# Sparse attention: order of the query parts, the key compression and the second key transposes

## The chip, the cores and the metric

One core of a Trainium2 chip runs the whole program in one launch. The metric is the device time of an execution in microseconds (us), lower is better. PE is TensorE, DVE is VectorE, ACT is ScalarE, POOL is GpSimd, and SP is SyncE, which issues the weight loads.

## The reference

The input x has 256 positions of width 1024 in float32. Three layers with a feed-forward part each are computed: a first block of forgetting attention and retention, then a layer of sparse attention (`nsa_pool_mixer`) with a pooling mixer, then a gated linear attention layer. The change lies in the sparse attention only. What it computes, for 8 query heads in 2 key groups of head dimension 64:

```python
h = x @ w_in                      # queries, six key/value sets, gates, u
kc = compress_blocks(k_cmp, ...)  # gelu(flat @ w1 + b1) @ w2: 15 compressed keys
vc = compress_blocks(v_cmp, ...)
p_c = masked_softmax(qb @ kc, ...);  o_c = p_c @ vc      # branch over compressed keys
p_s = masked_softmax(qb @ k_sel, ...); o_s = p_s @ v_sel # branch over selected blocks
p_w = masked_softmax(qb @ k_w, ...);  o_w = p_w @ v_w    # branch over the window
o = g0 * o_c + g1 * o_s + g2 * o_w
```

With 256 positions the selected blocks and the window both cover all keys, so both of these branches are causal attention over 256 keys, with different key sets.

## The kernel before

Every large product runs in three matmul passes, over a high and a low part of both factors: hi x hi, lo x hi, hi x lo. Weights stream in tiles of 128 x 1024 (512 KB) into a ring of 6 raw slots (SP, `fetch_w`). ACT makes the high part `whi` of each tile (line 600), DVE the low part `wlo` (line 1137), also in rings of 6, and PE uses both (lines 1816 to 1818, 12 matmuls for a tile of 256 input rows). The low part of a tile frees its raw slot for the next load.

The sparse attention's input product takes 16 such tiles, T_AIN + 0 to T_AIN + 15, four for each block of output columns: keys and values of compression and selection (tiles 0 to 3), queries (4 to 7), window keys, values and gates (8 to 11, 280 columns), and u (12 to 15). The work of the attention itself is written by hand between these tiles. Each engine has a table `between` (PE) or `tiles(...)` (ACT and DVE) whose entry n lists the steps that follow tile n in program order. On ACT and DVE the entry n comes after the high or low part of tile n + 3, except for entries 12 to 14, which come before it. Every engine runs its list in order, and semaphores alone join the lists.

The names that the change touches:

- `nsa_transposes(f)` on PE (line 2292): four 128 x 128 transposes into bank 2 or 3 of the PSUM tensor AT. f = 0, 1 are the keys and values to be compressed, 2 the window keys' set for the first branch, 3 to 6 the queries (position half t, head half j), 7 the second set of keys. f = 7 writes bank 2, and waits until DVE has copied the turned probabilities of group 6 out of it (`at_trd`). f = 5 and 6 wait until the low part before the last was taken from their bank (`nt_lo`).
- `nt_out(f)`, `q_out(f)` on ACT (line 941): copy of the transposed bank to SBUF as high part. `q_low(f)`, `k_low(f)` on DVE (lines 1547, 1553): its low part, read from the same bank.
- `compress` on PE (line 2320) is the product with w1, `hidden_bias` on ACT adds b1, `gelu_start` on DVE begins the gelu. `gelu_exp` on ACT (line 959) is the exponential in it, the first since other functions were used, so a table load stands with it. `gelu_end` on DVE (lines 1563 to 1567) ends it. `compress2` on PE (lines 2326, 2327) waits for it and forms the compressed keys and values. `compressed_out` on DVE (lines 1575 to 1580) copies them out.
- `cmp_scores` on PE (line 2336) are the scores on the compressed keys, `cmp_max` on DVE (to line 1604), `cmp_exp` on ACT (line 970) and `cmp_probs` on DVE (from line 1608) are their softmax, `cmp_transposes` on PE turns it.
- Groups 6 to 17 are the softmax groups of the other two branches. For group n: `S_(n)` scores on PE (lines 2041, 2052), always in bank 1 of AT, so that it waits for the exponentials of group n - 1; `maxima(n)` on DVE (line 1376); `exps(n)` on ACT (line 811); `weigh(n)` on DVE (lines 1622 to 1626); `T_(n)` transposes on PE (line 2065) into bank 2; `probs_out(n)` on DVE (line 1384), the copy out of it; `V_(n)` values on PE (lines 2390, 2394). Group 6 needs all four query parts (`nt_lo` at 5), and `T_(7)` waits for `k_low(7)` (`nt_lo` at 6), because both use bank 2.

Of the kernel before, what the change touches and what calls it, by code (L numbers as in the profile page):

```python
# [12 lines left out]
P = 128  # L13
# [157 lines left out]
def block_program(nc, dram, out):  # L171
    with ExitStack() as ctx:
        def sb(name, shape, dt=F32):
            return ctx.enter_context(nc.sbuf_tensor(name, shape, dt))
# [22 lines left out]
        kst = sb("kst", [P, 4, 512], F32R)  # L197
# [116 lines left out]
        K_HI = (2, 0)  # L314
# [18 lines left out]
        def rows_of(t):  # L333
            return slice(t * P, (t + 1) * P)
# [246 lines left out]
        def _(act):  # L581
# [221 lines left out]
            def exps(n):  # L803

                br, t, heads = GROUPS[n]
                act.wait_ge(at_max, n + 1)
                if n >= 2:
                    act.wait_ge(at_tr, n - 1)
                w = 512 // len(heads)
                for u, h in enumerate(heads):  # L810
                    ins = nc.scalar.activation(pr[:, n % 2, u * w:(u + 1) * w], AT[:, S_BANK[n], u * w:(u + 1) * w],
                                               ACT.Exp, bias=nmax[:, n % 2, u:u + 1],
                                               accum_out=rsum[:, t, 8 * br + h:8 * br + h + 1])
                ins.then_inc(at_exp, 1)
# [122 lines left out]
            def nt_out(f, dst, n=64):  # L937

                act.wait_ge(nt_tr, f + 1)
                b = AT[0:n, 2 if f == 7 else 2 + f % 2, :]  # L940
                nc.scalar.activation(dst, b if len(dst.shape) == 2 else b.rearrange("d (h s) -> d h s", h=4),
                                     ACT.Copy).then_inc(nt_done, 1)

            def q_out(f):
                t, j = (f - 3) // 2, (f - 3) % 2
                nt_out(f, q_tile(j, t), P)
# [47 lines left out]
            def nsa_hi(t):  # L994
# [9 lines left out]
                4: [lambda f=f: nt_out(f, kT[:, f * 512:(f + 1) * 512], P) for f in range(2)],  # L1004
                5: [lambda: nt_out(2, kst[:, K_HI[0], :], P)],
                7: [queries_out, hidden_bias],
                8: [gelu_exp] + [lambda f=f: q_out(f) for f in (3, 4)],
                9: [lambda f=f: q_out(f) for f in (5, 6)],
                10: [lambda: exps(6)],
                11: [window_out, branch_gates, lambda: exps(7)],  # L1010
                12: [lambda: exps(8)],
                13: [cmp_exp, lambda: nt_out(7, kst[:, K_HI[1], :], P), lambda: exps(9)],
                14: [cmp_out, lambda: exps(10)],
                15: [u_out, lambda: exps(11), means_out, lambda: exps(12), pooled_hi, lambda: exps(13)],
            }, range(12, 15))
# [94 lines left out]
        def _(dve):  # L1110
# [56 lines left out]
            def tiles(s0, s1, after, first=()):  # L1167


                for s in range(s0, s1):  # L1170
                    if s - s0 not in first:
                        raw_to(raw_of(s + LEAD) + 1)
                    for step in after.get(s - s0, ()):
                        step()
                    lo_to(s + LEAD)
# [194 lines left out]
            def maxima(n):  # L1370

                u = len(GROUPS[n][2])
                dve.wait_ge(at_mm, n + 1)
                if n >= 2:
                    dve.wait_ge(at_exp, n - 1)
                nc.vector.tensor_reduce(nmax[:, n % 2, 0:u], AT[:, S_BANK[n], :].rearrange("p (u k) -> p u k", u=u),
                                        AX, ALU.max, negate=True).then_inc(at_max, 1)
# [164 lines left out]
            def q_low(f):  # L1542

                t, j = (f - 3) // 2, (f - 3) % 2
                dve.wait_ge(nt_done, f + 1)
                own = q_tile(j, t)[64:P]
                tt(own, AT[64:P, 2 + f % 2, :].rearrange("d (h s) -> d h s", h=4), own.bitcast(F32), ALU.subtract)\
                    .then_inc(nt_lo, 1)

            def k_low(f, br):  # L1550

                dve.wait_ge(nt_done, f + 1)
                tt(kst[:, K_HI[br] + 1, :], AT[:, 2, :], kst[:, K_HI[br], :].bitcast(F32), ALU.subtract).then_inc(nt_lo, 1)
# [80 lines left out]
            def pooled_lo():  # L1634
# [4 lines left out]
                        hT_hi[:, 4 + g, :].bitcast(F32), ALU.mult, ALU.subtract).then_inc(pl_lo, 1)  # L1639

            tiles(T_AIN, T_AOUT, {
                5: [block_keys, lambda: k_low(2, 0)], 7: [gelu_start], 8: [gelu_end, lambda: q_low(3), lambda: q_low(4)],
                9: [compressed_out, lambda: q_low(5), lambda: q_low(6)],
                10: [lambda: maxima(6)],
                11: [gates_out, lambda: weigh(6), lambda: maxima(7)],
                12: [lambda: maxima(8), lambda: probs_out(6), lambda: weigh(7), cmp_max],
# [145 lines left out]
        def _(pe):  # L1792
# [353 lines left out]
            def fox_values(n):  # L2146

                if n == 0:
                    pe.wait_ge(bank_free[1], 4)
                if n == 2:  # L2150
                    pe.wait_ge(at_out, 1)
                _, t, heads = GROUPS[n]
                pe.wait_ge(at_trd, n + 1)
                b = 0
                for h in heads:
                    for kt in range(t + 1):
                        ins = mm(AT[:, 3, 64 * h:64 * h + 64], prT[:, n % 2, b * P:(b + 1) * P],
                                 proj[:, kt, FV + 64 * h:FV + 64 * (h + 1)], start=kt == 0, stop=kt == t)
                        b += 1
                ins.then_inc(at_pv, 1)  # L2160
# [53 lines left out]
            S_, T_, V_ = fox_scores, prob_transposes, fox_values  # L2214
# [77 lines left out]
            def nsa_transposes(f):  # L2292

                if f < 3:
                    pe.wait_ge(bank_free[0], 2 * (B_AIN // 2) + 2)
                    srcs = [acc[:, KD + 256 * t + P * g:KD + 256 * t + P * (g + 1)] for g in range(2) for t in range(NT)]
                    if f < 2:
                        srcs = [proj[:, t, KDUP + P * (2 * f + g):KDUP + P * (2 * f + g + 1)] for g in range(2) for t in range(NT)]
                elif f < 7:
                    t, j = (f - 3) // 2, (f - 3) % 2  # L2300
                    pe.wait_ge(bank_free[1], 2 * ((B_AIN + 1) // 2) + 2)
                    srcs = [acc[:, QD + D * t + P * (4 * j + a):QD + D * t + P * (4 * j + a + 1)] for a in range(4)]
                else:
                    pe.wait_ge(bank_free[0], 2 * ((B_AIN + 2) // 2) + 2)
                    pe.wait_ge(at_trd, NF + 1)
                    srcs = [acc[:, KD + 256 * t + P * g:KD + 256 * t + P * (g + 1)] for g in range(2) for t in range(NT)]
                if 2 <= f < 7:
                    pe.wait_ge(nt_done, f - 1)
                if 4 <= f < 7:
                    pe.wait_ge(nt_lo, f - 3 if f > 4 else 1)  # L2310
                for c, a in enumerate(srcs):
                    ins = nc.tensor.transpose(AT[:, 2 if f == 7 else 2 + f % 2, c * P:(c + 1) * P], a, ident)
                ins.then_inc(nt_tr, 1)
# [16 lines left out]
            def cmp_scores(tiles):  # L2330
                pe.wait_ge(c2_done, 3)
                pe.wait_ge(nt_lo, 5)
                for t in tiles:
                    for h in range(8):
                        for part in range(2):
                            ins = mm(AT[:, 0, 256 + P * t + 16 * h:256 + P * t + 16 * (h + 1)],
                                     q_stack(h)[:, rows_of(t)],
                                     kcst[:, part, h // 4, :], start=part == 0, stop=part == 1)
                ins.then_inc(cs_mm, 1)
# [72 lines left out]
            def pool_mix():  # L2412

                pe.wait_ge(pm_done, 2)
                for g in range(4):
                    ins = mm(PJ[:, 2 + g // 2, (g % 2) * S:(g % 2 + 1) * S], acc[:, POOLW + P * g:POOLW + P * (g + 1)],
                             proj[:, 1, RT_ + S * g:RT_ + S * (g + 1)], start=True, stop=True)
                    if g % 2:
                        ins.then_inc(py_mm, 1)

            S_, T_, V_ = nsa_scores, nsa_probs, nsa_values
# [3 lines left out]
                9: [lambda: nsa_transposes(5), lambda: nsa_transposes(6), compress2],  # L2425
                10: [lambda: S_(6)],
                11: [lambda: S_(7), lambda: cmp_scores((0,))],
                12: [lambda: T_(6), lambda: S_(8), lambda: cmp_scores((1,))],
                13: [lambda: V_(6), lambda: nsa_transposes(7), lambda: S_(9), lambda: T_(7)],
                14: [lambda: V_(7), cmp_transposes, lambda: T_(8), lambda: S_(10)],  # L2430
                15: [cmp_values, lambda: V_(8), lambda: T_(9), lambda: S_(11), pool_bands, lambda: V_(9), lambda: T_(10), lambda: S_(12),
                     pool_mix, lambda: V_(10), lambda: T_(11), lambda: S_(13)],
            }
            mixer(B_AIN, T_AIN, 3, quarters(3, from_x, (2, 3), [(mod_row, 8)]), [n for _, n in A_IN], between)
            between = {0: [lambda: V_(11), lambda: T_(12), lambda: S_(14)],
                       1: [lambda: V_(12), lambda: T_(13), lambda: S_(15)],
# [149 lines left out]
```

## Time and profile before

| | us |
|---|---|
| runs of the kernel before | 991.39, 990.47, 992.85 (median 991.39) |
| the profiled execution | 991.15 |
| its span, first to last instruction | 989.2 |
| the sparse attention's tiles and steps | about 380 to 475 of the span |

The profile gives the busy time of each engine and a chain of work that ended last, followed back from the last instruction. A timeline lists the instructions of an engine in order of time, those alike merged, with the idle time ahead of them and what ended it in brackets. Of the matmuls the starts are measured and the ends modelled, so distances are best taken from start to start. The granted clock is the share of TensorE's full clock of 2.4 GHz.

### The profile page before, as it was taken

What the parts mean: (1) busy time and instruction counts of PE and PEld (TensorE: products, weight loads), DVE (VectorE), ACT (ScalarE), POOL (GpSimd) and SP (SyncE); (2) the same over time, 40 slices, a digit from 0 to 9 for tenths busy, and PEclk for the clock granted to TensorE, in tenths of its full rate; (3) what the DMA queues carried; (4) which work ended last, traced back from release to release, by engine and by line L of the source; (5) the groups of instructions that cost most, each with busy time, mean ns of one, the idle gap of its engine ahead of it and who ended that gap; (6) DMA issues with size and microseconds to landing.
All of it is one profiled execution on the core that took longest, in us unless ns stands there. A gap on an engine that the chain in (4) does not pass through costs nothing.

```text
span 989.2 us, 13707 instructions
## 1 busy us (share of the span) xinstructions
PE 958.2 (97%) x4982; PEld 797.0 (81%) x4982; DVE 675.2 (68%) x875; ACT 463.4 (47%) x710; POOL 55.0 (6%) x61
## 2 busy tenths in 40 slices
PE   9999999999999999899899999998999999999996
PEld 7778877888888887777688888887776888888885
DVE  5868898895566576677976556667643876655657
ACT  5477535464445345544355444444652434544441
POOL 3040111200000001000200000000000010000000
PEclk9999999999999999999999999999999999999998
DMA  9979787596555676421375665564342537566541
GB/s 303 336 227 276 220 255 235 198 313 210 194 170 193 206 258 165 128 86 46 121 246 192 196 204 174 190 211 153 127 148 86 168 132 233 193 197 205 170 148 43
DMA packets 110053, 186.91 MB, mean 189 GB/s; under 512 B 8729, under 2 KB 67169, under 8 KB 109985
## 3 DMA queue, kind: packets, MB, share of 16 engines
q1 hardware_dynamic: 104800, 177.33, 55.1%
q0 software_dynamic: 2656, 8.54, 3.2%
q8 instruction: 32, 0.52, 0.2%
q10 hardware_dynamic: 2544, 0.35, 0.2%
q14 instruction: 21, 0.16, 0.1%
HBM read 185.15 MB, written 1.05 MB: 188 GB/s over the span
## 4 chain that ended last, share of the span: by engine, by line
PE 78%; DVE 11%; ACT 3%; issue 3%; DMA 2%; POOL 2%; SPq 0%; POOLq 0%; DVEq 0%; ACTq 0%
PE AT L1956 16%; PE PJ L1816 14%; PE PJ L1817 14%; PE PJ L1818 14%; PE AT L1960 8%; DVE wlo L1137 3%; POOL rstd L483 2%; ACT whi L600 1%; PE AT L1802 1%; DVE bn L1225 1%; DMA raw<-in_w_out_dram 1%; DMA raw<-in_w_ada_dram 1%; PE AT L1816 1%; PE AT L2065 1%; DVE x L1223 1%
## 5 line engine op out<-in xcount | busy, mean ns | idle before, releaser
L1137 DVE TENSOR_TENSOR wlo<-raw,whi 128x1024 fp32r<-128x1024 f32 x144 | 173.4, 1221 | 50.9 <-ACT whi L600 50.1
L1956 PE MATMUL AT<-hT,whi 128*128 128x512 f32 x720 | 179.5, 391 | 0.0
L1263 DVE TENSOR_TENSOR wlo<-raw,whi 128x1024 fp32r<-128x1024 f32 x144 | 169.6, 1219 | 0.0
L600 ACT ACTIVATE whi<-raw 128x1024 fp32r<-128x1024 f32 x144 | 146.6, 1054 | 40.1 <-DMA raw<-in_w_in_dram 28.8
L1816 PE MATMUL PJ<-whi,uhi 128*128 128x512 f32 x392 | 154.0, 393 | 0.4
L1817 PE MATMUL PJ<-wlo,uhi 128*128 128x512 f32 x392 | 153.0, 390 | 0.0
L1818 PE MATMUL PJ<-whi,ulo 128*128 128x512 f32 x392 | 152.6, 389 | 0.0
L1956 PEld LDWEIGHTS AT<-hT,whi 128*128 128x128 f32 x720 | 131.9, 188 | 25.3
L1816 PE MATMUL PJ<-whi,hT 128*128 128x512 f32 (+1 forms) x360 | 146.7, 407 | 4.7 <-DVE hT L1320 1.6
L1273 DVE TENSOR_TENSOR pr<-AT,pr 128x512 f32<-128x512 f32 x45 | 31.1, 691 | 169.0 <-ACT pr L655 169.0
L647 ACT ACTIVATE whi<-raw 128x1024 fp32r<-128x1024 f32 x144 | 140.7, 1049 | 0.3 <-DMA raw<-in_mlp_w_dram 0.3
L1817 PE MATMUL PJ<-wlo,hT 128*128 128x512 f32 (+1 forms) x360 | 139.6, 388 | 0.0
L1818 PE MATMUL PJ<-whi,hT 128*128 128x512 f32 (+1 forms) x360 | 139.5, 388 | 0.0
L655 ACT ACTIVATE pr<-AT 128x512 f32<-128x512 f32 x45 | 26.8, 595 | 173.4 <-PE AT L1960 173.4
L1960 PEld LDWEIGHTS AT<-hT,wlo 128*128 128x128 f32 x720 | 98.2, 190 | 7.0
L1960 PE MATMUL AT<-hT,wlo 128*128 128x256 f32 x720 | 100.4, 282 | 0.0
L1818 PEld LDWEIGHTS PJ<-whi,ulo 128*128 128x128 f32 x392 | 73.6, 188 | 15.7
L1816 PEld LDWEIGHTS PJ<-whi,hT 128*128 128x128 f32 x360 | 68.2, 189 | 22.2 <-issue 4.8
L1816 PEld LDWEIGHTS PJ<-whi,uhi 128*128 128x128 f32 x392 | 73.7, 188 | 15.2 <-issue 1.2
L1817 PEld LDWEIGHTS PJ<-wlo,uhi 128*128 128x128 f32 x392 | 73.8, 188 | 13.8 <-issue 0.2
L1818 PEld LDWEIGHTS PJ<-whi,hT 128*128 128x128 f32 x360 | 68.0, 189 | 14.4
L1817 PEld LDWEIGHTS PJ<-wlo,hT 128*128 128x128 f32 x360 | 68.2, 189 | 13.0 <-issue 1.0
(332 smaller groups left out, 995.9 us busy)
## 6 DMA issues: line engine op xcount, KB each, us to landing
raw<-in_mlp_w_dram SPq DMA_DIRECT2D x128, 512.0 KB, 4.8
raw<-in_w_in_dram SPq DMA_DIRECT2D x32, 512.0 KB, 6.4
raw<-in_w_ada_dram SPq DMA_DIRECT2D x32, 512.0 KB, 5.6
raw<-in_w_mlp_in_dram SPq DMA_DIRECT2D x32, 512.0 KB, 4.9
raw<-in_w_mlp_out_dram SPq DMA_DIRECT2D x32, 512.0 KB, 4.7
raw<-in_c_w_in_dram SPq DMA_DIRECT2D x24, 512.0 KB, 4.5
raw<-in_w_ada_dram SPq DMA_DIRECT2D x32, 256.0 KB, 6.6
raw<-in_a_w_in_dram SPq DMA_DIRECT2D x12, 512.0 KB, 5.2
```

Of the source, the lines that this page charges most:

```text
L483: nc.gpsimd.tensor_tensor(rstd[:, col:col + n], stat[:, col:col + n], nhalf[:, 0:n], ALU.pow).then_inc(rstd_ready, 1)
L600: nc.scalar.activation(whi[:, s % SPL, :], raw_slot(r), ACT.Copy).then_inc(hi_done, 1)
L647: nc.scalar.activation(whi[:, s % SPL, :], raw_slot(r), ACT.Copy).then_inc(hi_done, 1)
L655: nc.scalar.activation(pr[:, 0, :].rearrange("p (f s) -> p f s", f=2), AT[:, up_banks(j), S:], ACT.Copy).then_inc(cross_out, 1)
L1137: tt(wlo[:, n % SPL, :], raw_slot(r), whi[:, n % SPL, :].bitcast(F32), ALU.subtract).then_inc(raw_done, 1)
L1263: tt(wlo[:, s % SPL, :], raw_slot(r), whi[:, s % SPL, :].bitcast(F32), ALU.subtract)\
L1273: tt(z, AT[:, up_banks(j), 0:S], z, ALU.add).then_inc(up_out, 1)
L1816: mm(o, a, hi, start=start, stop=False)
L1817: mm(o, a, lo, start=False, stop=False)
L1818: return mm(o, b, hi, start=False, stop=stop)
L1956: mm(out(f), whi[:, s % SPL, c(kk, f)], hT[:, k, :, :].rearrange("p a s -> p (a s)"), start=k == 0, stop=False, skip_group_check=True)
L1960: ins = mm(out(f)[:, 0:S], wlo[:, s % SPL, c(kk, f)], hT_hi[:, k, :], start=False, stop=k == KC - 1, skip_group_check=True)
```

## The change

Three tables are reordered. On ACT, entry 8 runs the copies of query parts 3 and 4 before the gelu's exponential, and entry 13 the copy of the second set of keys before the exponential of the compressed scores. On DVE, entry 8 takes the low parts of query parts 3 and 4 before `gelu_end`, and entry 9 those of parts 5 and 6 before `compressed_out`. On PE, the transposes of the second set of keys go from entry 13, behind the values of group 6, to the end of entry 12, ahead of tile 13. No instruction is added or removed.

```diff
@@ ACT
-                8: [gelu_exp] + [lambda f=f: q_out(f) for f in (3, 4)],
+                8: [lambda f=f: q_out(f) for f in (3, 4)] + [gelu_exp],
                 9: [lambda f=f: q_out(f) for f in (5, 6)],
                 10: [lambda: exps(6)],
                 11: [window_out, branch_gates, lambda: exps(7)],
                 12: [lambda: exps(8)],
-                13: [cmp_exp, lambda: nt_out(7, kst[:, K_HI[1], :], P), lambda: exps(9)],
+                13: [lambda: nt_out(7, kst[:, K_HI[1], :], P), cmp_exp, lambda: exps(9)],
@@ DVE
-                5: [block_keys, lambda: k_low(2, 0)], 7: [gelu_start], 8: [gelu_end, lambda: q_low(3), lambda: q_low(4)],
-                9: [compressed_out, lambda: q_low(5), lambda: q_low(6)],
+                5: [block_keys, lambda: k_low(2, 0)], 7: [gelu_start], 8: [lambda: q_low(3), lambda: q_low(4), gelu_end],
+                9: [lambda: q_low(5), lambda: q_low(6), compressed_out],
@@ PE
-                12: [lambda: T_(6), lambda: S_(8), lambda: cmp_scores((1,))],
-                13: [lambda: V_(6), lambda: nsa_transposes(7), lambda: S_(9), lambda: T_(7)],
+                12: [lambda: T_(6), lambda: S_(8), lambda: cmp_scores((1,)), lambda: nsa_transposes(7)],
+                13: [lambda: V_(6), lambda: S_(9), lambda: T_(7)],
```

## Rows read from the trace of the kernel before

**Rows 1.** The page: busy time and share of PE; chain that ended last, by engine.

```profile
PE 958.2 (97%) x4982; PEld 797.0 (81%) x4982; DVE 675.2 (68%) x875; ACT 463.4 (47%) x710; POOL 55.0 (6%) x61
...
PE 78%; DVE 11%; ACT 3%; issue 3%; DMA 2%; POOL 2%; SPq 0%; POOLq 0%; DVEq 0%; ACTq 0%
```

**Rows 2.** PE's waits, 385 to 475 us: what for; us, times, longest.

```profile
PE AT L2312 <- DVE uhi L1547: 1.0, 1, 1.0
PE AT L2041 <- DVE ulo L1547: 0.9, 1, 0.9
```

**Rows 3.** Timeline of ACT: start, duration, instruction, idle before and releaser.

```profile
403.01 1.28 ACT L959 ACT_TABLE_LOAD   x1
404.31 0.25 ACT L959 ACTIVATE sc<-sc 64x60 f32<-64x60 f32 x1
404.47 0.58 ACT L941 ACTIVATE uhi<-AT 128x512 fp32r<-128x512 f32 x1
404.94 0.58 ACT L941 ACTIVATE ulo<-AT 128x512 fp32r<-128x512 f32 x1
...
407.37 0.60 ACT L941 ACTIVATE uhi<-AT 128x512 fp32r<-128x512 f32 x1 [0.90 <-PE AT L2312]
...
426.01 0.40 ACT L970 ACTIVATE proj<-proj 128x240 f32<-128x240 f32 x1 [1.49 <-DVE proj L1604]
```

**Rows 4.** Timeline of DVE, same columns.

```profile
404.59 0.18 DVE L1563 TENSOR_SCALAR sc<-sc 64x60 f32<-64x60 f32 x1 [0.34 <-ACT sc L959]
...
405.86 0.69 DVE L1547 TENSOR_TENSOR uhi<-AT,uhi 64x512 fp32r<-64x512 f32 x1
...
407.19 1.23 DVE L1137 TENSOR_TENSOR wlo<-raw,whi 128x1024 fp32r<-128x1024 f32 x1
408.55 0.17 DVE L1575 CAST kcst<-nhalf 128x4 fp32r<-128x4 f32 x1
...
412.42 0.69 DVE L1376 TENSOR_REDUCE nmax<-AT 128x4 f32<-128x512 f32 x1
...
421.83 0.69 DVE L1376 TENSOR_REDUCE nmax<-AT 128x2 f32<-128x512 f32 x1 [2.39 <-PE AT L2052]
422.44 0.68 DVE L1384 COPY prT<-AT 128x512 f32<-128x512 f32 x1
...
428.18 0.69 DVE L1553 TENSOR_TENSOR kst<-AT,kst 128x512 fp32r<-128x512 f32 x1 [1.06 <-ACT kst L941]
...
429.62 0.69 DVE L1384 COPY prT<-AT 128x512 f32<-128x512 f32 x1 [0.15 <-PE AT L2065]
```

**Rows 5.** Timeline of PE, same columns.

```profile
403.12 1.03 PE L2312 MATMUL AT<-cst,acc 128*128 128x128 f32 x8
...
406.70 1.24 PE L2312 MATMUL AT<-cst,acc 128*128 128x128 f32 x8 [1.01 <-DVE uhi L1547]
407.87 0.40 PE L2326 MATMUL AT<-sc,nsm 64*128 64x30 f32 x2
...
414.70 0.39 PE L2041 MATMUL AT<-negb,identb 128*128 128x512 bf16 x1 [0.74 <-ACT pr L811]
...
423.33 0.48 PE L1816 MATMUL PJ<-whi,hT 128*128 128x512 f32 x1
...
427.38 0.72 PE L2052 MATMUL AT<-kst,uhi 128*128 128x256 f32 x4
428.92 0.66 PE L2065 MATMUL AT<-cst,pr 128*128 128x128 f32 x4 [0.83 <-DVE kst L1553]
```

**Rows 6.** Windows: length, busy PE, PEld, DVE, ACT, POOL; granted clock; DMA share, GB/s.

```profile
133.00:136.00 3.00, 0.93 (x6) 0.53 (x6) 2.60 (x6) 0.60 (x1) 0.00 (x0) 1.00 0.56 214
136.00:140.00 4.00, 4.00 (x17) 3.61 (x18) 4.00 (x4) 2.74 (x4) 0.00 (x0) 0.57 0.41 117
70.00:72.00 2.00, 0.19 (x4) 0.00 (x0) 1.09 (x2) 0.92 (x1) 2.00 (x3) 1.00 0.30 115
72.00:76.00 4.00, 3.76 (x22) 3.20 (x23) 3.76 (x5) 3.10 (x3) 0.45 (x1) 1.00 0.79 211
```

## The prediction

> **What bounds the kernel now.** I read the engine table of the page first: PE is busy for 958.2 us of the span, 97% [rows 1]. The chain that ended last lies on PE for 78% and on DVE for 11% [rows 1]. So a change of order on ACT and DVE can only win where PE waits for one of them. The list of PE's waits between 385 and 475 us, the stage that the diff touches, and then the bracketed idle times in PE's own timeline name four such stops: 1.0 us in front of transposes for DVE's `q_low`, 0.9 us in front of group 6's scores for `q_low` [rows 2], 0.74 us in front of group 7's scores for ACT's exponentials, and 0.83 us in front of a transpose for `k_low` [rows 5]. That is 3.5 us, 0.35% of the run, and the most that this change could return here. The timelines of ACT, DVE and PE around these four stops give the order behind each [rows 3 to 5]. "Tile n" is weight tile T_AIN + n, "group n" a softmax group.
>
> **First part: `gelu_exp`, `gelu_end` and `compressed_out` go behind the `q_out`/`q_low` pairs.** Nothing is added or removed; the same instructions stand in another order. Before, ACT runs the table load (1.28 us from 403.01), the exponential (404.31), then `q_out(3)` and `q_out(4)` (404.47, 404.94) [rows 3]. DVE runs `gelu_end` from 404.59, `q_low(3)` and `q_low(4)` from 405.86, the low part of tile 12 from 407.19, `compressed_out` from 408.55, then `q_low(5)`, `q_low(6)`, the low part of tile 13, and the maxima of group 6 at 412.42 [rows 4].
>
> ACT in the new order. PE's transposes 3 and 4 start at 403.12 [rows 5]. From the start of such transposes to the copy that reads them it is 0.67 us (406.70 to 407.37) [rows 3, 5], so `q_out(3)` starts at 403.79. `q_out(4)` follows 0.47 later, the pitch of this pair when both inputs are there (404.47 to 404.94) [rows 3]: 404.26, end 404.84 with its 0.58. Load and exponential keep their distances (403.01 to 404.31 is 1.30) [rows 3]: the load starts at 404.86, the exponential at 406.16.
>
> DVE in the new order. `q_low(3)` runs from 404.39 and `q_low(4)` to about 405.7, so PE's transposes 5 and 6 start when tile 9 ends, 1.01 us (their stop) sooner than 406.70 [rows 5]: this stop is gone. But `gelu_end` starts 0.28 behind the exponential (404.31 to 404.59) [rows 3, 4], at 406.44, and ends 1.24 later at 407.68. PE's `compress2` waits for it and stood at 407.87 before [rows 5]: it gains only 0.1 us. The first stop isn't removed; it moves behind the two transposes (1.17 us from 405.69) and is there near 1 us again. On DVE, `gelu_end` is 1.85 later than 404.59; the pair's 1.33 (405.86 to 407.19) no longer stands behind it; and the gap of 0.13 between the low part of tile 12 (end 407.19 + 1.23) and 408.55 closes [rows 4]. So everything from there on is 1.85 - 1.33 - 0.13 = 0.39 later, the maxima of group 6 too: 412.8 in place of 412.42. I take +0.38.
>
> The scores of group 6 do come sooner: `q_low(6)` ends at 406.44 + 1.27 + 1.26 + 1.31 = 410.3, by the pitches of `gelu_end`, a low part and a pair [rows 4], so PE wins about 0.8 of the second stop. It has nothing to spend it on. After tile 11 it must issue the scores of group 7 into the same bank, and these wait for the exponentials of group 6, which wait for the maxima, which stand on DVE behind the low part of tile 13 whatever the scores do. From the maxima at 412.42 to the scores at 414.70 [rows 4, 5] all shifts by +0.38. The stop of 0.74 grows to 0.74 + 0.8 + 0.38 = 1.9 us. **First part: a loss of 0.38 us.**
>
> The bounds. If `q_out(4)` came 0.60 after `q_out(3)`, the length of a copy as at 407.37 [rows 3], it would be 0.51; if the table load stayed in front of the copies, `gelu_end` would start behind the `q_low` pair at 406.24, a loss of 0.2. I take the pitch of 0.47 as it is the same two copies. If PE's 0.8 us counted after all, the part would be a gain of 0.8. What is queued behind the later steps: on ACT the high part of tile 12, about 1.0 later, on DVE its low part, 0.5 later than 407.19 [rows 4], which PE needs at tile 12, behind the scores of group 7 at 414.70 [rows 5]; on SP the fetch into the slot that this low part frees, 0.5 later too, and in this stage PE waits for no DMA [rows 2]. All are costed at nothing; with the cover gone they would cost 0.5. POOL has no step here. From 414.70 to tile 13 at 423.33 PE's timeline shows no stop [rows 5], since what it waits for shifts alike, so the 0.38 is carried there whole.
>
> The Trainium skill, ScalarE: Activation LUTs, section "Step-by-step: what each stage is for", says that the load of a table set stands right before the activation that needs it; the row agrees (403.01, 404.31) [rows 3]. The same page, section "What ACT_TABLE_LOAD costs", adds a drain of 1.38 us to a load of 1.28. The row shows the load, and ACT not idle ahead of it [rows 3]; with that drain the first part would cost 1.76 us, an estimate by that page.
>
> **Second part: `nsa_transposes(7)` goes from behind tile 13 to ahead of it, and `nt_out(7)` ahead of `cmp_exp`.** In its new place it waits on PE for DVE's copy of group 6's turned probabilities, which leaves bank 2 of AT free. That copy ends at 422.44 + 0.68 = 423.12, and PE starts tile 13 at 423.33 [rows 4, 5]; both carry the same +0.38. PE starts 0.15 behind such a releaser (405.86 + 0.69 = 406.55 to 406.70) [rows 4, 5], so it would start at 423.27: cost 0, at most 0.1. Queued behind this wait is all of tile 13. The four transposes take as long in either place. ACT copies them in its hole of 1.49 us ahead of `cmp_exp` (426.01) [rows 3], and DVE's `k_low(7)` starts as soon as the low part of tile 15 ends, 1.06 sooner than 428.18 [rows 4]. On PE, the scores of group 9 stay at 427.38, since the transposes only changed sides of tile 13, and group 7's transposes lose their stop of 0.83 [rows 5]. DVE sets what comes next: its maxima of group 9 start 0.04 after the scores' end at 427.38 + 0.72 [rows 5], at 428.14, the copy 0.61 later (421.83 to 422.44) at 428.75, against 429.62 [rows 4]: 0.87. Its softmax over the compressed keys and its weighing hang on that copy, and PE's next transposes on them. Bounds 0.83 and 0.95. **Second part: a gain of 0.87 us.**
>
> **Sum.** 0.38 - 0.87 = -0.49 us, say -0.5. The profiled execution took 991.15 us (the span of 989.2 and 1.95 around it), the runs shown have a median of 991.39. On the profile's base that is 990.65, on the median's 990.9.
>
> **The rivals.**
> - *The scores' head start counts in full.* The first part is then a gain of 0.8, and the sum -1.7: 989.7. It needs the maxima at 411.6, and against that stands DVE's queue, which has no hole from 406.44 on. Chance 0.07.
> - *The second set's transposes stall.* If the copy out of bank 2 came so late that the stop only moved ahead of tile 13, the second part would give nothing: +0.4, 991.8. For it: the margin is under 0.1 us. Chance 0.08.
> - *A drain at the table load.* The exponential would come another 1.38 later, and the sum be +0.9: 992.3. Against it: no gap stands ahead of 403.01 [rows 3]. Chance 0.06. The page named above is what speaks for it.
> - *TensorE's clock falls.* The place is the two stops that the new order makes, over 1 us near 406.4 and 1.9 us near 413.2. Between 133 and 136 us PE was busy for 0.93 of 3 us, and the granted clock over the next 4 us was 0.57, mostly the 1.2 GHz level [rows 6]: (1 - 0.57) x 4 = 1.7 us lost. Against it: between 70 and 72 us PE was busy for 0.19 of 2 us, and the clock stayed at 1.00 [rows 6]. [...] One fall gives -0.5 + 1.7 = +1.2: 992.6, chance 0.15. A fall at each stop gives +2.9: 994.3, chance 0.04. This is the case that ends slower.
>
> **Numbers.** The forecast has 0.60. The range goes from 989.7, the first rival, to 992.9, one fall with 0.3 of scatter; outside are the double fall and the tails. About 0.2%, 2.0 us, is what a measurement here can tell from no change. Only the double fall, or one fall with a drain or with scatter, gets there: slower 0.08. Faster by 2.0 us would need the first rival with scatter: 0.05. Within: 0.87.
>
> **What would show it.** ACT's table load at 404.9 behind two copies; PE's transposes 5 and 6 an us sooner and a stop in front of `compress2`, which is near 407.8; the scores of group 6 at 410.3; group 7's at 415.1, with a stop near 1.9 for ACT; the copy for `k_low(7)` ahead of `cmp_exp`; group 7's transposes at 428.3 in place of 428.92 [rows 5], with no stop for `k_low(7)`. A granted clock under 1.00 between 407 and 420, a table load ahead of the copies, maxima of group 6 before 412.4, or a stop in front of `nsa_transposes(7)` would each make the sum wrong.

## The result, and the profile after

| | kernel before | changed kernel |
|---|---|---|
| median of 18 runs, us | 992.42 | 995.22 |
| lowest and highest, us | 989.95, 994.93 | 990.63, 998.12 |
| profiled execution, us | 991.15 | 996.75 |
| its span, us | 989.2 | 994.8 |
| its mean granted clock | 0.993 | 0.987 |

The changed kernel is slower by 0.24%: the ratio is 1.0024, 95% interval 1.0013 to 1.0035, that is 2.4 us with 1.3 to 3.5. The forecast of 990.9 us had its range end at 992.9, and 995.22 lies outside.

The waits of PE in this stage come first (385 or 388 us to 480; what waits for what; us in total, times, longest). After:

```profile
PE AT L2041 <- ACT pr L811: 1.7, 1, 1.7
PE AT L2326 <- DVE proj L1567: 1.2, 1, 1.2
PE AT L2065 <- issue: 0.9, 3, 0.4
PE PJ L1816 <- DVE hT L1638: 0.4, 1, 0.4
```

The two waits of [rows 2] are gone, and so is the 0.83 for `k_low` in [rows 5]. In their place stand 1.2 us in front of `compress2` and 1.7 in front of group 7's scores (0.74 before). Both were forecast. The listed waits are shorter than before as a sum, so they don't say where 2.4 us went. The windows do (start and end; length; busy time of PE, PEld, DVE, ACT, POOL; granted clock; DMA share; GB/s):

```profile
410.00:412.00 2.00, 0.84 (x7) 0.66 (x6) 1.90 (x5) 2.00 (x4) 0.00 (x0) 1.00 0.32 120
412.00:416.00 4.00, 3.91 (x30) 3.66 (x31) 3.87 (x9) 0.81 (x1) 0.00 (x0) 1.00 0.42 131
416.00:419.00 3.00, 1.30 (x12) 1.05 (x10) 0.67 (x2) 2.30 (x9) 0.00 (x0) 1.00 0.50 173
419.00:423.00 4.00, 4.00 (x22) 4.00 (x22) 3.64 (x8) 1.31 (x6) 0.00 (x0) 0.53 0.34 114
423.00:426.00 3.00, 3.00 (x8) 2.32 (x9) 0.00 (x0) 1.50 (x8) 0.00 (x0) 0.50 0.07 25
426.00:430.00 4.00, 4.00 (x32) 3.71 (x31) 1.56 (x5) 0.90 (x4) 0.00 (x0) 0.99 0.00 0
```

Behind the stop of 1.7 us the granted clock is at 0.50, the 1.2 GHz level, from 419 to 426 us. PE is fully busy there, at half the clock. In the profile of the kernel before, the clock was 1.00 through the whole stage. The product of time and missing clock is 0.47 x 4 + 0.50 x 3 + 0.01 x 4 = 3.4 us. I call this the clock loss below; for a whole run it is (1 - mean granted clock) x span. In this stage a stretch at 0.50 (a fall) has, in every profile that shows one, a clock loss of either 1.7 us, a single fall, or 3.4 us, a double one.

PE's timeline after, around this stop (start, duration, instruction, idle before):

```profile
406.67 1.04 PE L2312 MATMUL AT<-cst,acc 128*128 128x128 f32 x8
...
411.28 0.40 PE L2326 MATMUL AT<-sc,nsm 64*128 64x30 f32 x2 [1.16 <-DVE proj L1567]
...
413.75 0.39 PE L2041 MATMUL AT<-negb,identb 128*128 128x512 bf16 x1
...
418.26 0.39 PE L2041 MATMUL AT<-negb,identb 128*128 128x512 bf16 x1 [1.70 <-ACT pr L811]
418.30 1.29 PE L2052 MATMUL AT<-kst,ulo 128*128 128x128 f32 x8
419.39 1.82 PE L2336 MATMUL AT<-kcst,uhi 128*128 128x16 f32 x8
421.06 1.85 PE L2336 MATMUL AT<-kcst,ulo 128*128 128x16 f32 x8
422.77 0.77 PE L1816 MATMUL PJ<-whi,hT 128*128 128x512 f32 x1
```

Eight matmuls of the compressed scores (line 2336) take 1.82 us here. The start of the stage itself is 3.55 us later than before (406.67 against 403.12 in [rows 5]). That lies in code that the change doesn't touch, and most of it goes with falls of the clock at other places: ahead of this stage the changed kernel's profile has four single falls, that of the kernel before two. So the stage is measured from the start of the transposes of query parts 3 and 4. The three marks that I use rest on these rows, with [rows 5] and the timeline above. Before:

```profile
411.15 0.39 PE L2041 MATMUL AT<-negb,identb 128*128 128x512 bf16 x1 [0.91 <-DVE ulo L1547]
411.19 1.19 PE L2052 MATMUL AT<-kst,uhi 128*128 128x128 f32 x8
...
437.32 1.95 PE L2360 MATMUL AT<-proj 120*128 120x128 f32 x16
```

After:

```profile
442.88 1.95 PE L2360 MATMUL AT<-proj 120*128 120x128 f32 x16
```

| from the start of transposes 3 and 4, us | before | after |
|---|---|---|
| scores of group 6 | 8.03 | 7.08 |
| scores of group 7 | 11.58 | 11.59 |
| values of the compressed branch (line 2360, behind tile 15) | 34.20 | 36.21 |

### The profile page after: what moved, and what is told of

Its sections match the earlier page's. It is cut to its first block, busy times and chain, and to the rows that moved or that the text cites. A ratio compares the mean times of both kernels' runs of the same rounds, so it can differ in the third digit from the quotient of the medians.

```text
span 994.8 us, 13707 instructions
## 1 busy us (share of the span) xinstructions
PE 963.5 (97%) x4982; PEld 802.3 (81%) x4982; DVE 674.5 (68%) x875; ACT 463.4 (47%) x710; POOL 55.0 (6%) x61
## 4 chain that ended last, share of the span: by engine, by line
PE 79%; DVE 11%; issue 3%; ACT 3%; DMA 2%; POOL 2%; SPq 0%; POOLq 0%; DVEq 0%; ACTq 0%
PE AT L1956 16%; PE PJ L1816 14%; PE PJ L1817 14%; PE PJ L1818 14%; PE AT L1960 8%; DVE wlo L1137 3%; POOL rstd L483 2%; ACT whi L600 1%; PE AT L1802 1%; DMA raw<-in_w_out_dram 1%; DVE bn L1225 1%; PE AT L2065 1%; DMA raw<-in_w_ada_dram 1%; DMA raw<-in_w_in_dram 1%; PE AT L1816 1%
```

## The experiments

Theory **"clock"**: the new order makes a long stop in front of group 7's scores, TensorE's clock falls behind it, and this costs more than the order brings. Rival **"queues alone"**: the order costs time through DVE or ACT, and the fall is chance. All kernels were run with 12 timed runs each, beside 17 to 35 of the kernel before on the same chip. The last two columns are of the one profiled execution: the clock loss between 412 and 427 us, and the distance to the values of the compressed branch.

| kernel | median, us | ratio to before (95%) | mean clock loss of the runs, us | fall in the stage, us | distance, us |
|---|---|---|---|---|---|
| before (116 runs) | 992.75 | | 8.3 | 0 | 34.20 |
| changed (18 runs) | 995.22 | 1.0024 (1.0013 to 1.0035) | 11.9 | 3.4 | 36.21 |
| e10 changed, again | 993.49 | 1.0025 (1.0009 to 1.0041) | 11.1 | 3.4 | 36.20 |
| e1 first part only | 995.05 | 1.0019 (1.0003 to 1.0035) | 10.4 | 3.4 | 37.22 |
| e2 second part only | 992.62 | 0.9998 (0.9982 to 1.0014) | 9.5 | 0 | 33.23 |
| e3 scores' stop filled | 991.94 | 0.9992 (0.9976 to 1.0009) | 8.6 | 1.7 | 34.57 |
| e4 maxima first | 991.38 | 0.9991 (0.9971 to 1.0010) | 9.6 | 1.7 | 33.60 |
| e5 before, delayed | 995.88 | 1.0037 (1.0022 to 1.0052) | 10.8 | 3.4 | 38.26 |
| e6 before, delayed, filled | 995.17 | 1.0018 (1.0003 to 1.0033) | 8.8 | 1.7 | 36.61 |
| e7 compress2's stop filled | 993.98 | 1.0022 (1.0005 to 1.0039) | 11.3 | 1.7 | 34.55 |
| e8 candidate | 991.79 | 0.9992 (0.9977 to 1.0006) | 9.0 | 0 | 32.29 |
| e9 both stops filled | 992.58 | 1.0004 (0.9990 to 1.0019) | 9.4 | 1.7 | 34.56 |
| e11 second part, filled | 990.57 | 0.9983 (0.9965 to 1.0001) | 7.3 | 0 | 33.22 |
| e12 before, filled | 992.76 | 0.9997 (0.9980 to 1.0014) | 7.9 | 1.7 | 35.50 |

The mean clock loss has a standard error of 0.5 to 0.9 us for 12 runs, 0.2 for the 116 of before. No version is shown to be faster than the kernel before: no interval lies wholly below 1.

### The parts alone: e1 and e2

e1 takes the ACT entry 8 and the DVE entries 8 and 9 of the change, e2 the ACT entry 13 and the PE entries.

> Only the first part: the exponential of the gelu behind query copies 3 and 4 on ScalarE, gelu_end and compressed_out behind the low parts on VectorE; the second set of keys stays where it was. Theory 'clock': the stop of PE in front of group 7's scores grows from 0.7 to about 1.7 us, the granted clock falls to half behind it as in the changed kernel (from 419 to 426 there), and that costs about 3.4 us: 992.4 + 0.4 + 3.4 = 996.2 us, 0.4% slower than before. Theory 'queues alone': the maxima of group 6 are 0.4 us later, no more, the clock is as before: 992.8 us, the same.

Measured: 995.05 us, ratio 1.0019; that is 1.2 us under what "clock" expected, and the kernel is slower than before, which "queues alone" did not expect. The stop and the fall are those of the changed kernel, in PE's timeline and in the windows of e1:

```profile
418.49 0.39 PE L2041 MATMUL AT<-negb,identb 128*128 128x512 bf16 x1 [1.71 <-ACT pr L811]
```

```profile
419.00:423.00 4.00, 4.00 (x23) 4.00 (x22) 3.41 (x8) 1.55 (x6) 0.00 (x0) 0.54 0.28 92
423.00:427.00 4.00, 4.00 (x13) 3.22 (x13) 0.23 (x1) 1.51 (x8) 0.00 (x0) 0.60 0.11 41
```

> Only the second part: the transposes of the second set of keys one step up on PE, their copy ahead of cmp_exp on ScalarE. Both theories: the stop of 0.83 us in front of group 7's transposes is gone, the stop in front of group 7's scores stays at 0.74, no fall of the clock in this stage: 992.4 - 0.9 = 991.5 us. If the second part itself were what brings the loss, it would be 994 or more.

Measured: 992.62 us, no difference by the runs; the 0.9 that was expected is inside the interval (1.6 us to each side). The order itself shows in the trace without scatter: the distance to the compressed values is 33.23 us in place of 34.20, a gain of 0.97, and no fall in the stage. So the loss is in the first part, and its profile has the fall: its distance of 37.22 us is 34.20 + 3.02, so by order it gives or takes nothing.

### Filling the stops: e3, e7, e9

A filler is a matmul of constants, 128 x 256, 0.44 us, into a bank of AT that nobody uses at that point (`busy`). It changes no other instruction. e3:

```diff
-                11: [lambda: S_(7), lambda: cmp_scores((0,))],
+                11: [lambda: busy(3, 3), lambda: S_(7), lambda: cmp_scores((0,))],
```

> The changed kernel with three matmuls of 256 columns on constants, written to an unused bank, ahead of group 7's scores on PE, so that PE works in the stop of 1.7 us. Theory 'clock': no fall of the clock near 419, time 995.2 - 3.4 = 991.8 us, as the forecast of the queues alone has it (-0.5 against before). Theory 'queues alone' (the loss is a delay on DVE or ACT): the fillers save nothing, 995.2 us; and if they stood in the way of the scores, up to 0.3 more.

Measured: 991.94 us. The scores of group 7 stand at 11.60 us behind the transposes, so the fillers cost nothing, and the stop has shrunk to 0.4. The runs' mean clock loss is 8.6 us, against 8.3 before and 11.6 in the 30 runs of the changed kernel. That is what "clock" expects, and "queues alone" is out: with the order unchanged, some 3 us come back. But the profiled execution still has a fall, a single one, and it starts later, some 3.9 us behind the start of group 7's scores in place of 0.9:

```profile
411.00:415.00 4.00, 3.61 (x26) 3.11 (x24) 2.25 (x3) 1.71 (x9) 0.00 (x0) 1.00 0.49 158
415.00:419.00 4.00, 4.00 (x30) 3.77 (x30) 3.06 (x8) 1.90 (x6) 0.00 (x0) 0.97 0.33 92
419.00:423.00 4.00, 4.00 (x17) 3.13 (x16) 0.58 (x1) 1.50 (x8) 0.00 (x0) 0.61 0.24 87
```

Its loss is 0.03 x 4 + 0.39 x 4 = 1.7 us, half of the changed kernel's. The fillers don't rule out every fall in this stage.

e7 has fillers in the other stop alone:

```diff
-                9: [lambda: nsa_transposes(5), lambda: nsa_transposes(6), compress2],
+                9: [lambda: nsa_transposes(5), lambda: nsa_transposes(6), lambda: busy(1, 2), compress2],
```

> The changed kernel with two matmuls on constants ahead of compress2, in the stop of 1.16 us, and none ahead of group 7's scores. If the clock falls by the stop in front of group 7's scores alone, it still falls: 995.2 us. If it takes both stops together, this filling is worth as much as the other one was: 992 us.

Measured: 993.98 us, between the two that were expected; but the ratio is 1.0022 and the mean clock loss 11.3, as in the changed kernel. The stop in front of `compress2` went from 1.16 to 0.29, the one of 1.7 stayed, and by the runs the loss stayed too. So the stop in front of group 7's scores is the one that counts. Its profile, of the fastest of its runs, has a single fall that starts 2.9 us behind the start of group 7's scores, not the double one, so the stop near 410 may have a share; one profile doesn't settle it.

> The changed kernel with fillers in both stops: two matmuls on constants ahead of compress2, three ahead of group 7's scores, order unchanged. From the traces, the order alone is worth -1.0 us (first part 0.0, second -1.0), so with the clock of the kernel before (0.992): 992.7 - 1.0 = 991.7 us. Theory 'clock': that. If the changed order cost time by a way of its own, filling wouldn't bring it under 994.

e9 joins both edits. Measured: 992.58 us, 0.9 above what was expected and 0.6 above e3; mean clock loss 9.4 with an error of 0.7. It is under 994, but doesn't beat e3, so filling `compress2`'s stop brings nothing more that these runs can tell.

### The stop made by hand in the old order: e5, e6

```diff
-                10: [lambda: maxima(6)],
+                10: [lambda: nc.vector.tensor_reduce(dly[:, :], x[:, 0, :], AX, ALU.max), lambda: maxima(6)],
```

> The kernel before, with one extra reduction of 128 x 1024 on VectorE (about 1.1 us, into a word that nobody reads) ahead of the maxima of group 6; nothing else is changed. It makes the stop in front of group 7's scores some 1.1 us longer (0.74 to 1.85), as long as in the changed kernel, without any of its reordering. Theory 'clock': the mean granted clock is lower than in the kernel before by about as much as in the changed one (0.003), so that the time rises by more than the delay: 992.8 + 1.1 + 3 = 997, with a fall of the clock between 415 and 425 in the profile. Rival 'no tie between this stop and the clock': 992.8 + 1.1 = 993.9 us and the clock of the kernel before.

> The same with three matmuls on constants (0.44 us each) ahead of group 7's scores. The delay stays, the stop is filled. Theory 'clock': only the delay is left, 993.9 us, and the mean granted clock is that of the kernel before (0.992). Rival: no difference from the one without the fillers.

Measured: 995.88 and 995.17 us. In e5 the scores of group 7 come 1.07 us later than before, and the windows show the fall (PE's timeline, then the windows; line numbers are one higher in this kernel):

```profile
414.73 0.39 PE L2042 MATMUL AT<-negb,identb 128*128 128x512 bf16 x1 [1.82 <-ACT pr L812]
```

```profile
412.00:415.00 3.00, 1.18 (x10) 0.93 (x9) 1.13 (x2) 1.83 (x9) 0.00 (x0) 1.00 0.51 175
415.00:419.00 4.00, 4.00 (x24) 4.00 (x22) 3.17 (x8) 1.78 (x6) 0.00 (x0) 0.57 0.22 68
419.00:423.00 4.00, 4.00 (x13) 3.26 (x13) 0.46 (x1) 1.50 (x8) 0.00 (x0) 0.57 0.17 64
```

The distance of 38.26 us is 34.20 + 1.07 of delay + 2.99: the price of a double fall, in an order that nobody changed. Other pairs of profiles agree: 3.02 between e1 and before, 2.98 between the changed kernel and e2 for a double fall, 1.30 to 1.35 (e12 and before, e4 and e8, e3 and e11) for a single one. e6 keeps the delay and fills the stop; its fall is single and its distance 36.61, that is 34.20 + 1.07 + 1.34. The mean clock loss of the runs is 10.8 us unfilled, 8.8 filled, 8.3 in the kernel before. e5 is what "clock" expected, 1 us less. e6 was expected at 993.9 and came 1.3 higher in the median (0.9 in the mean); the clock loss fell as forecast, the time only partly, and the rest I can't place. By their times alone the two aren't told apart: the ratios' intervals overlap, and the means differ by 1.4 us with a standard error of 0.8. The clock loss differs by 2.0 with an error of 0.7.

### Taking the stop away by the order: e4 and e8

```diff
-            }, range(12, 15))
+            }, (10, 12, 13, 14))
```

in DVE's table: with entry 10 in this list, `maxima(6)` stands ahead of the low part of tile 13.

> The changed kernel with one more move on VectorE: the maxima of group 6 ahead of the low part of tile 13 instead of behind it. Theory 'the low part of tile 13 stands in the way': the maxima come 1.1 us sooner against the scores of group 6, the stop in front of group 7's scores shrinks from 1.7 to about 0.6 us, the clock doesn't fall there, and the time is 991.8 - 1.1 = 990.7 us. Rival 'the stop is set by something else': the stop stays near 1.7, the clock falls, 995.2 us.

Measured: 991.38 us. The stop is 0.75, and the scores of group 7 are at 10.63 in place of 11.59 (timelines of DVE and of PE):

```profile
412.75 0.69 DVE L1376 TENSOR_REDUCE nmax<-AT 128x4 f32<-128x512 f32 x1
413.36 1.22 DVE L1137 TENSOR_TENSOR wlo<-raw,whi 128x1024 fp32r<-128x1024 f32 x1
```

```profile
415.04 0.39 PE L2041 MATMUL AT<-negb,identb 128*128 128x512 bf16 x1 [0.75 <-ACT pr L811]
```

It was DVE's queue that stood between the early scores of group 6 and their use, as the prediction had it. The time is 0.7 us above what was expected, and that the clock doesn't fall in the stage didn't come: a single fall is in this profile, from 2.9 us behind the start of group 7's scores.

> The changed kernel, with the maxima of group 6 ahead of the low part of tile 13 on VectorE, two matmuls on constants ahead of compress2 and one ahead of group 7's scores. By the queues: -1.8 us against the kernel before (first part +0.4, second -0.9, maxima -1.2), by the clock nothing lost: 992.8 - 1.8 = 991.0 us or a little less, with no fall of the clock between 400 and 425. Rival 'the clock falls here whatever fills the stops' (a fall was seen in the profile of the version with fillers ahead of the scores alone): 991.4 as without the fillers, mean clock 0.990.

e8 adds two fillers ahead of `compress2` and one ahead of group 7's scores. Measured: 991.79 us, 0.8 above the expected. No fall in the stage, and the shortest distance of all, 32.29 us, 1.91 under the kernel before. Over the whole run only about 1 us of it is seen, ratio 0.9992 (0.9977 to 1.0006). The profiled execution is the fastest of the twelve, 988.63 us at a mean clock of 0.995, and the twelve have 0.991; so that the fillers keep the clock up in the other runs isn't shown, and the rival (991.4 us, 0.990) isn't ruled out.

### Repeat, and the fillers in the old order: e10, e11, e12

> The changed kernel itself once more, beside the others on one chip, for the mean granted clock and the place of the falls: 995.2 us, mean clock 0.988 against 0.992 of the kernel before, and a fall between 415 and 427 us.

Measured: 993.49 us, 1.7 under the expected median; the mean is 994.45, against 992.49 of the kernel before on that chip. The ratio is 1.0025, the mean clock 0.989, and again there is the double fall at the same place, in its windows:

```profile
412.00:416.00 4.00, 2.30 (x19) 2.05 (x18) 1.66 (x2) 2.30 (x9) 0.00 (x0) 1.00 0.42 136
416.00:420.00 4.00, 4.00 (x23) 3.90 (x23) 3.64 (x8) 1.31 (x6) 0.00 (x0) 0.58 0.33 105
420.00:424.00 4.00, 4.00 (x12) 3.14 (x11) 0.00 (x0) 1.50 (x8) 0.00 (x0) 0.57 0.07 26
```

The distance is 36.20, after 36.21 in the first profile: with the clock's part known, the stage repeats within 0.01 us.

> Only the second part, with the three stops of the old order filled: two matmuls on constants ahead of the transposes of query part 5, one ahead of group 6's scores, one ahead of group 7's. By the queues 992.7 - 1.0 = 991.7 us. If falls in this stage also hit the kernel before in some of its runs, filling its stops gives a little more: the clock rises over 0.992, and the time is 991 or less. If not, it is the same as without fillers.

> The kernel before in its own order, with the same four fillers in its three stops as in the last one (two ahead of the transposes of query part 5, one ahead of group 6's scores, one ahead of group 7's). It parts the gain of 1.8 us of that version (990.9 mean against 992.7) into order and clock. If the kernel before loses clock in this stage in some of its runs, the mean granted clock rises over 0.992 and the time falls to about 992; if it doesn't, both stay: 992.7 us, clock 0.9917. The order alone is no faster here: nothing is moved.

e11 is the second part and `busy(1, 2)` ahead of transposes 5, `busy(1, 1)` ahead of group 6's scores, `busy(3, 1)` ahead of group 7's; e12 has the fillers without the second part. Measured: 990.57 us and 992.76 us. e12 is the kernel before within its scatter, clock loss 7.9 against 8.3, and its profile even has a single fall between 418 and 423 us. So filling the old stops brings nothing that can be told, and the single fall isn't bound to a stop in front of group 7's scores, which is 0.31 us here. e11 has the lowest median of all, ratio 0.9983 (0.9965 to 1.0001): the second part's 1.0 us by the trace, and a low clock loss that may be chance. It beats the changed kernel; that it beats the kernel before isn't shown, since its interval just reaches past 1.

## Why the prediction was wrong

**The mechanism was in it, with the wrong chance.** The rival "TensorE's clock falls" named the place, the stop in front of group 7's scores. It got 0.15 for one fall and 0.04 for two, and the sum put the clock at nothing. In the profiles, each of the two executions of the changed kernel has a double fall there, and so has e1, which shares the order of the first part, and e5, which shares only the stop. The 30 timed runs of the changed kernel have a mean clock loss of 11.6 us against 8.3. The step that failed is this term, left at nothing on the evidence against it: that between 70 and 72 us PE was busy for 0.19 of 2 us "and the clock stayed at 1.00" [rows 6]. This was one execution. In the profile of the changed kernel the same stop, in code that no edit touches, is 2.04 us long (PE's timeline), and this time the clock falls (windows):

```profile
74.15 1.57 PE L2132 MATMUL AT<-cst,proj 128*64 128x128 f32 x8 [2.04 <-DVEq L1361]
```

```profile
70.00:74.00 4.00, 2.11 (x14) 1.09 (x13) 2.13 (x5) 2.83 (x4) 4.00 (x4) 1.00 0.57 208
74.00:78.00 4.00, 3.85 (x14) 3.22 (x15) 3.81 (x4) 2.90 (x3) 0.37 (x1) 0.57 0.77 210
```

This stop is 2.04 to 2.06 us long in all 14 profiles. The clock falls behind it (between 72 and 78 us) in eight and holds in six. Behind the stop of 1.66 us near 136, whose fall [rows 6] shows, it falls in ten and holds in four. So such a stop is a risk that some executions pay and others don't, and one profile in which it isn't paid says little of the chance.

**What belongs to the long stop.** With a stop of at most 0.75 us in front of group 7's scores, none of the nine profiles has a double fall in the stage; five have a single one, which starts 2.4 to 3.9 us behind the start of these scores. With a stop of 1.7 to 1.8 us left open, four of five have a double fall, which starts within 0.7 to 1.4 us of them. So what the long stop brings is the early, double fall. What brings the later, single one no run here shows.

**The price of a fall.** The 1.7 us of [rows 6] is right as a unit: it comes once or twice in each fall. The prediction priced a fall per stop, two of them at 3.4 us, which with the order's -0.5 gave its +2.9. What came was a double fall behind one stop. In time it costs 2.99 us (e5) and a single one 1.34 (e6), less than the clock loss; the likely reason, not tested, is that not all of PE's time in it scales with the clock.

**The first part: 0.38 us forecast, 0.0 measured.** Group 7's scores are at 11.58 before and 11.59 after. ACT's side came as worked out: table load and exponential behind both copies, `gelu_end` at 409.99, which is 3.32 behind the transposes, as forecast (406.44 - 403.12). The mis-sized term is what follows on DVE. Its timeline after:

```profile
411.01 0.21 DVE L1567 COPY proj<-sc 64x120 f32<-64x120 f32 x1
411.15 1.21 DVE L1137 TENSOR_TENSOR wlo<-raw,whi 128x1024 fp32r<-128x1024 f32 x1
412.39 0.69 DVE L1547 TENSOR_TENSOR uhi<-AT,uhi 64x512 fp32r<-64x512 f32 x1
...
413.72 0.17 DVE L1575 CAST kcst<-nhalf 128x4 fp32r<-128x4 f32 x1
...
414.85 1.22 DVE L1137 TENSOR_TENSOR wlo<-raw,whi 128x1024 fp32r<-128x1024 f32 x1
415.98 0.68 DVE L1376 TENSOR_REDUCE nmax<-AT 128x4 f32<-128x512 f32 x1
```

The maxima start 1.13 us behind the low part of tile 13. The prediction shifted the whole queue rigidly from 412.42 on [rows 4], as if the maxima had stood there for DVE. In the kernel before they stand 1.30 behind the low part of tile 13 (from 411.12) and had waited for the scores of group 6, whose matmuls end at 412.38 (411.19 + 1.19, above); that distance was a wait and not DVE's pitch. In e5 the extra reduction, which needs nothing of PE, starts 1.14 behind the same low part. With the scores early these 0.17 us close up. Two more distances are shorter with another instruction behind them: from the last step of `gelu_end` to the next instruction 0.14 in place of 0.24, and from the start of `compressed_out` to what follows it 1.13 in place of 1.24. Why, the runs don't show. Together that is 0.38 us, the whole of the forecast's loss.

**The second part: 0.87 forecast, 0.97 measured** (34.20 to 33.23 in e2), just over its upper bound of 0.95. The missing 0.10 is in "The four transposes take as long in either place": from their start to the next instruction it is 0.41 us ahead of tile 13 (e2) and was 0.50 behind the values of group 6, so the scores of group 9 come 0.10 sooner. The other steps came: no stop in front of the moved transposes, the copy ahead of `cmp_exp`, `k_low(7)` straight behind the low part of tile 15.

**The rivals.** That the scores' head start counts in full didn't come; e4 shows what it would have taken. The stall of the moved transposes didn't come. Nor did the drain: ACT's rows after, the copy of query part 4, the load and the exponential, are

```profile
407.80 0.59 ACT L941 ACTIVATE ulo<-AT 128x512 fp32r<-128x512 f32 x1
408.41 1.28 ACT L959 ACT_TABLE_LOAD   x1
409.70 0.25 ACT L959 ACTIVATE sc<-sc 64x60 f32<-64x60 f32 x1
```

The load starts 0.02 after the copy ends. The Trainium skill, ScalarE: Activation LUTs, section "What ACT_TABLE_LOAD costs", gives 1.28 us for the load, with which the row agrees, and 1.38 for a drain, which neither order shows; the measurement decides.

**The sum.** By order alone the change is worth 0.0 - 0.97 = -1.0 us, twice the -0.49 of the forecast. The measured +2.4 us is that and a clock loss that is higher by 3.3 us in the mean (11.6 against 8.3), which is 2.9 us of time if 3.4 costs 3.0: +1.9, inside the interval of 1.3 to 3.5. A double fall in every run of the changed kernel, and none before, would give -1.0 + 3.0 = +2.0. That all of the 3.3 is lost in this stage isn't shown; that fillers ahead of group 7's scores bring 3.0 of it back (e3) speaks for it.

**The base.** The three runs shown had a median of 991.39 us; 116 runs have 992.75. The scatter of the kernel before, 989.4 to 997.2, goes with its mean granted clock (the correlation of time and clock loss is 0.79 over the 116 runs); in the 14 profiles the code that no edit touches has its falls at different places. So the base of the forecast was 1.0 to 1.4 us too low.

What stays open: why a long stop gives a double fall in four of five profiles and a single one in e7; what the single falls come from; and how often the place is hit, since only a profile shows the place, and there is one for each kernel.

## What to carry to other kernels

Where PE is the bound and an order on the other engines is changed, list not only how long PE waits in all, but how long the longest stop gets: here the order was 1.0 us better and the run 2.4 us slower, because two stops, of 0.91 and 0.74, became one of 1.7 and the clock fell behind it. An early result is worth nothing while the engine that must take it up has something else ahead in its queue, so move the consumer along with the producer (e4), or fill the stop with harmless matmuls (e3). Here either took the loss back; a gain over the kernel before isn't shown for them. And a distance between two instructions may only be shifted as a pitch when one has seen that the second didn't wait for another engine.

## What the runs showed of the hardware

Unexpected was how closely the scatter between executions goes with the clock: the correlation of time and clock loss is 0.91 over the 30 runs of the changed kernel. The same program, with the same stops, had a mean granted clock between 0.985 and 0.993 over 18 of them, and took 990.63 us at 0.993 against 998.12 at 0.985. Leaving out the last 10 us of the run, where PE runs out of work, every fall in the 14 profiles had a clock loss of 1.7 or 3.4 us: behind a stop of 2.06 us the clock held in one execution, and behind the same stop of 2.04 us it fell in another. Fillers that cut the stop of 1.7 us to 0.39 took the mean clock loss from 11.6 to 8.6 us (e3).
